# Releasing a split weight chunk with the next chunk's first product, in a decoder-trunk step on one core

## What is computed

```python
def chunk_gmlp(x, w_in, b_in, lnv_g, lnv_b, w_s, b_s, w_out):
    z = jax.nn.gelu(x @ w_in + b_in)              # w_in: 1024 x 2048
    u, v = jnp.split(z, 2, axis=-1)
    v = layer_norm(v, lnv_g, lnv_b)
    ...
    s = jnp.einsum('gts,ncsgd->nctgd', w_mix, vc) + b_s[:, :c].T[None, None, :, :, None]
    ...
    return (u * s) @ w_out, v

def proj_heads(x, w):                             # w_k, w_v, b_w_q: 1024 x 1024
    return (x @ w).reshape(x.shape[0], x.shape[1], N_HEADS, -1)
```

## Time and profile before

| | |
|---|---|
| runs before | 1445.66, 1441.37, 1445.92 us; median 1445.66 |
| profiled execution | 1442.07 us, its span 1440.2 us |
| granted TensorE clock, mean | 0.903 |
| TensorE products | 1210.9 us busy, 84% |
| TensorE weight loads | 934.6 us, 65%, beside the products |
| VectorE | 944.4 us, 66% |
| ScalarE | 697.9 us, 48% |
| GpSimd | 255.9 us, 18% |
| first projections | 15 to 127 us |
| first expert layer | about 175 to 565 us |
| K, V and Q | about 600 to 768 us |

### The profile page before, as it was taken

The page is one execution under the profiler, slowest core; times in us unless marked ns, Lnnn a source line. Parts: engine busy times, 40 slices in busy tenths (PEclk is TensorE's granted clock), DMA queues, the critical chain, the costliest instruction groups (busy, mean ns, idle before and its releaser), DMA issues.

```text
span 1440.2 us, 16770 instructions
## 1 busy us (share of the span) xinstructions
PE 1210.9 (84%) x5776; PEld 934.6 (65%) x5776; DVE 944.4 (66%) x1148; ACT 697.9 (48%) x748; POOL 255.9 (18%) x261
## 2 busy tenths in 40 slices
PE   6979982899999994499999999989819999999920
PEld 4755771678888883277776666667717788888810
DVE  4466567598888885833423445465656988888845
ACT  4341222577777784222113544332316777777721
POOL 2021040231111231400000000010313311112223
PEclk9989975899999997699998999989659999999965
DMA  9212157189999987533321123324362999999741
GB/s 347 95 59 95 56 188 261 47 319 372 373 370 378 377 316 266 208 91 119 130 79 59 47 101 118 118 92 145 123 246 77 362 373 369 370 372 373 295 156 62
DMA packets 142513, 302.55 MB, mean 210 GB/s; under 512 B 11872, under 2 KB 12032, under 8 KB 142336
## 3 DMA queue, kind: packets, MB, share of 16 engines
q1 hardware_dynamic: 123008, 250.23, 48.9%
q0 software_dynamic: 19168, 51.31, 10.0%
q10 hardware_dynamic: 288, 0.36, 0.1%
HBM read 288.36 MB, written 30.28 MB: 221 GB/s over the span
## 4 chain that ended last, share of the span: by engine, by line
PE 47%; DVE 7%; ACT 2%; DMA 1%; issue 1%; POOL 0%; POOLq 0%; DVEq 0%; ACTq 0%; SPq 0%; PEldq 0%
PE ps L1450 10%; PE ps L1452 10%; PE ps L1451 10%; PE ps L1721 3%; PE ps L1784 2%; PE ps L1769 2%; PE ps L1738 1%; DVE x L1248 1%; PE ps L1755 1%; PE ps L1525 1%; PE ps L1647 1%; PE ps L1473 1%; DVE wl L870 1%; PE ps L1730 1%; ACT wh L614 1%
## 5 line engine op out<-in xcount | busy, mean ns | idle before, releaser
L870 DVE TENSOR_TENSOR wl<-raw,wh 128x2048 fp32r<-128x2048 f32 x210 | 480.9, 2314 | 208.9 <-ACT wh L614 205.3
L614 ACT ACTIVATE wh<-raw 128x2048 fp32r<-128x2048 f32 x210 | 398.3, 1915 | 181.6 <-PE ps L1452 124.7
L1450 PE MATMUL ps<-wh,xgTh 128*128 128x512 f32 x512 | 209.7, 410 | 6.7 <-DVE xgTl L1198 5.7
L1452 PE MATMUL ps<-wh,xgTl 128*128 128x512 f32 x512 | 204.2, 399 | 0.0
L1451 PE MATMUL ps<-wl,xgTh 128*128 128x512 f32 x512 | 203.5, 397 | 0.0
L1450 PE MATMUL ps<-wh,xTh 128*128 128x512 f32 x448 | 184.2, 411 | 12.1 <-DVE u L939 9.2
L1452 PE MATMUL ps<-wh,xTl 128*128 128x512 f32 x448 | 179.1, 400 | 0.0
L1451 PE MATMUL ps<-wl,xTh 128*128 128x512 f32 x448 | 179.0, 400 | 0.0
L1450 PEld LDWEIGHTS ps<-wh,xgTh 128*128 128x128 f32 x512 | 97.4, 190 | 35.9 <-DVE wl L870 8.2
L1450 PEld LDWEIGHTS ps<-wh,xTh 128*128 128x128 f32 x448 | 86.3, 193 | 45.9 <-issue 22.2
L1450 PE MATMUL ps<-wh,hTh 128*128 128x512 f32 x256 | 105.4, 412 | 10.1 <-DVE hTl L1209 10.1
(11 more groups left out here) (266 smaller groups left out, 1715.5 us busy)
## 6 DMA issues: line engine op xcount, KB each, us to landing
raw<-in_moe_w_up SPq DMA_DIRECT2D x120, 1024.0 KB, 10.7
raw<-in_moe_w_down SPq DMA_DIRECT2D x62, 1024.0 KB, 11.9
raw<-in_a_w_in SPq DMA_DIRECT2D x8, 1024.0 KB, 20.6
ahead_up<-in_moe_w_up SPq DMA_DIRECT2D x8, 1024.0 KB, 8.9
yl<-y_rows POOLq DMA_DIRECT2D x8, 1024.0 KB, 8.5
raw<-in_cache_k SPq DMA_DIRECT2D x16, 512.0 KB, 4.4
raw<-in_cache_v SPq DMA_DIRECT2D x16, 512.0 KB, 4.9
raw<-in_a_w_out SPq DMA_DIRECT2D x4, 1024.0 KB, 5.0
```

What stands on the lines that cost most here:

```text
L614: act.activation(wh[:, slot], src, ACT.Copy).then_inc(high[key], 1)
L870: dve.tensor_tensor(wl[:, slot], src, wh[:, slot].bitcast(F32), ALU.subtract).then_inc(low[key], 1)
L1450: pe.matmul(out, high_, w_high, start=start, stop=False)
L1452: return pe.matmul(out, low_, w_high, start=False, stop=stop)
```

## The change

A chunk's release moves. `sample_chunk` gets an argument `behind`: with it, the first of its four products increments `used` for the chunk before. `project` passes it for the second half always, and for the first half in all projections but the first of each series (there the chunk before belongs to no `project`, or there is none). The increment behind the first half, and the wait and increment behind the second half, go; only the last projection of each series keeps the wait and the sequencer's increment (`last`).

```diff
-            def sample_chunk(key, n, kh, bank):
+            def sample_chunk(key, n, kh, bank, behind=False):
 
                 slot = landed(key, n)
                 for j in range(4):
                     mm = pe.matmul(ps[j * NSAMP:(j + 1) * NSAMP, bank], xTs[:, 4 * kh + j], raw[:, slot, j],
                                    start=(kh == 0), stop=(kh == 1))
+                    if behind and j == 0:
+                        mm.then_inc(used[key], 1)
                 mm.then_inc(sampled, 1)
...
-            def project(key, s0, m0, between=None):
+            def project(key, s0, m0, between=None, behind=True, last=False):
...
-                    sample_chunk(key, s, kh, (m0 + SAMP) % PROJ_BANKS)
+                    sample_chunk(key, s, kh, (m0 + SAMP) % PROJ_BANKS, behind or kh == 1)
...
-                    if kh == 0:
-                        mm.then_inc(used[key], 1)
-                    else:
-                        mm.then_inc(proj_done, 1)
-                        pe.wait_ge(proj_done, m0 + TILES)
-                        pe.sem_inc(used[key], 1)
+                mm.then_inc(proj_done, 1)
+                if last:
+                    pe.wait_ge(proj_done, m0 + TILES)
+                    pe.sem_inc(used[key], 1)
...
-                project("a", 2 * j, M_WIN + 5 * j)
+                project("a", 2 * j, M_WIN + 5 * j, None, j > 0, j == 3)
...
-                project("b", 2 * j, M_QKV + 5 * j, between)
+                project("b", 2 * j, M_QKV + 5 * j, between, j > 1, j == 5)
```

## The result

The changed kernel took 1436.19 us (median of six runs), the kernel before 1443.05 us (six runs, 1441.37 to 1445.92). One run of the changed kernel took 3151.6 us, for a reason that is not known, and is left out of the ratio; the other five lie from 1434.03 to 1437.11 us. The ratio of the means is 0.9945, with a 95% interval from 0.9929 to 0.9962: 0.55% faster, where no change was forecast. The profiled execution took 1436.21 us, 5.9 us less than the one before.

A forecast was written before the change was run, and what follows sets the result against it. TensorE paced K, V and Q, two releases the end of the first projections. First projections +1.4 us and K, V and Q -1.5 us gave -0.1 us: 1445.5 us, no change (0.83), range 1440.4 to 1448.3 us.

The forecast's parts named there:

- The drains: Seams between projections shrink to 0.33 us: 0.6 us saved in the first projections, 1.5 us in K, V and Q.
- The releases: Chunk releases come 0.98 us later; in the first projections +0.4 us at TensorE's restart, +1.4 us at mixing and transposes.
- the last row: Sign in the profile after: the spatial mixing's transposes start at about 143.3 us, against 141.89 us before.
- The rivals: Only drains count, 1443.6 us (0.12); seam does not close, 1447.6 us (0.10); four-way packing breaks, 1451.7 to 1458.6 us (0.07).
- The clock: TensorE's low-clock stretch after the 9.24 us stall in the fourth projection: no change, bounds 1.7 us either way.
- the sum: First projections +1.4 us and K, V and Q -1.5 us: -0.1 us in all.
- The base: The median of three runs before, 1445.66 us, from which the sum gave 1445.5 us.
- The rule on semaphores: Packed products end in order, so one increment on the last suffices; each further one adds about 26 ns to the tail.
- The estimate of 0.4 us: Loss by the semaphore rule for sixteen groups with two increments, making the sum +0.3 us instead of -0.1.

The follow-up runs named there:

- e2: The change in the four first projections only, K, V and Q as in the kernel before; 1443.58 us, ratio 1.0016.
- e5: The changed kernel plus six products nobody reads ahead of the fifth projection of K, V and Q; 1443.86 us.
- e10: The kernel of the early release, run and profiled once more; 1434.35 us.
- e6: The kernel before plus eight products nobody reads ahead of the fifth projection of K, V and Q; 1439.82 us, ratio 0.9989.
- e4: The kernel before plus 19 small products nobody reads, in two TensorE gaps around the start of attention; 1442.83 us, ratio 0.9999.
- the early release: Against the kernel before: no drain, first halves release their own chunk, for second halves ScalarE waits for the finished-products count; 1440.35 us, ratio 0.9991.

## Why the prediction was wrong

- **The drains: right.** Seven seams at 0.32 to 0.33 us. K, V and Q are shorter: from 0.96 us behind (650.91 to 651.87 us, the sample products of their second projection) to 0.82 us ahead (768.00 to 767.18, the last transposes) is 1.8 us; 1.5 were forecast, and the four seams alone give that.
- **The releases: right, the last row by luck.** "0.98 us later": ScalarE's split stands 79.42 - 77.95 = 1.47 us behind the start of the last big product 78.66 - 78.16 = 0.50 us before: 0.97 us. The trace's semaphore updates have the release 1.06 us behind the group's start; 1.05 were forecast. Without the 0.37 us that lie ahead of the first seam, the restart is 0.37 us late and the mixing 1.44 us; +0.4 and +1.4 were forecast. The transposes came at 143.22 us, 143.3 were forecast, but there two things cancel: the 0.37 us, and the mixing, which took 14.04 us instead of 14.52 (129.18 to 143.22, 127.37 to 141.89 us).
- **The rivals: none of the three happened.** The sample groups did not grow (1.00 us), the seams did close, and the releases did count.
- **The clock: the step that failed.** The prediction said, of the low stretch behind the stall in the first projections, "I take no change, and 1.7 us either way as its bounds". It treated that stretch as the only one the change could touch. That stretch kept its 10.2 us (in e2's profile it lasted 13.6). The kernel before had another one right behind the last seam, 774 to 788 us, at the start of attention, and the change moved the work by some 1.5 us against the clock's rise. It went, and with it 5.7 us (0.81 us ahead at the first scores, 6.49 at 941.60 us). That e5 brings it back and costs 7.6 us for 1.4 us of work shows that this, and not the sum, made the result. From there to the end of the span a part is given back: 1440.2 - 1434.4 = 5.8 us remain. Why the clock does not fall when the work stands 1.5 us earlier is open.
- **The base.** The forecast on the median, 1445.5 us, took 1445.66 us of three runs as its base; six runs gave 1443.05. Of the 9.3 us between forecast and result, 2.6 are this.
- **What could have been read beforehand.** The chain shows the score products at the start of attention with 1.57 us a pair where others of the same line take 0.84, and the granted clock of 774 to 788 us stood in the trace. A stretch behind the changed stage at half the clock, with TensorE busy all through, was worth 6 to 7 us; as a rival it would have had its price, though not its chance.
- **The rule on semaphores** of the Trainium skill ("TensorE: Matmul & The Clock Gate", section "The cost: per-tile semaphore tail") holds for the tail: by the trace's semaphore updates the last increment of a group comes 1.136 us behind the group's start in the changed kernel and 1.110 us in e10, where the group has one increment, 0.026 us later. But TensorE does not wait for it: the next product starts 1.00 us behind the group's start with one increment and with two. The estimate of 0.4 us on TensorE's path did not come true, and the sum without it was the right one.

## What to carry to other kernels

Where a kernel has stretches at the lower clock, a change of 1 us upstream can gain or lose several there, with no bearing on its own merit: list these stretches of the whole trace, with what the engine waited for ahead of each, and give every one behind the changed place a price in the prediction. To tell such a gain from the change's own, add the saved time back as work whose result nobody reads (e5), and look at the heaps of the single runs and at their granted clocks, not at the median alone. And a release that rides on the next product comes when that product ends: with a packed group of 1 us that is 1 us late, which is free only where the waiting engine has nothing pressing behind it.

## What the runs showed of the hardware that was not expected

- With eight more products half of the runs were faster than the median of the kernel before (e6: five of ten from 1437.7 to 1439.0 us, against 1442.63 us, where four of 31 lie under 1439); as a whole a gain is not shown.
- Filling the two short gaps ahead of the fall did not save it: the granted clock fell 114 us later instead, and the low stretch at the end of attention grew from 10 to 17 us (e4).
- The place of the work against the clock's rise is nearly the same in the profiles of a kernel (130.2 to 130.5 us in three of the one before, 128.7 and 128.8 of the changed one), although the rise itself lies anywhere between 639.6 and 642.0 us in them. It is not always so: the early release had 128.8 us twice and 130.1 us once, and the fall came with the 130.1.
- The first of four products packed side by side ends with the last: its increment comes 1.06 us behind the group's start, the last one's at 1.14.
